# Both token halves of a tile multiplied together, block by block, into two PSUM banks in turn

## What is computed

```
z = rmsnorm(x) @ w_in                      # 1024 -> 7 x 1024: u, v, B, C, h, gate_a, gate_b
v = layernorm(gelu(v));  a = gelu(u) * (tril(w_s[g]) mixed over 128 positions of v + b_s[g])
bconv = B * causal_conv3(C * h)
m = sigmoid(gate_a) * (a @ w_pa) + sigmoid(gate_b) * (bconv @ w_pb)
x = x + m @ w_o
x = x + (silu(xn @ w_gate) * (xn @ w_up)) @ w_down     # xn = rmsnorm(x)
y = rmsnorm(x)
```

## Time and profile before

| | |
|---|---|
| median of 3 runs | 960.77 us (960.02 to 961.20) |
| span of the profiled execution | 959.0 us (its own device time is not shown apart) |
| TensorE busy (matmul) | 924.1 us, 96%, 7269 matmuls |
| TensorE weight loads | 919.4 us, 7269 loads |
| VectorE, ScalarE, GpSimd busy | 525.2 us, 259.3 us, 85.4 us |
| chain that ended last, by engine | PE 94%, DVE 3%, DMA 1% |

### The profile page before, as it was taken

The page is one execution under the profiler, slowest core; times in us unless marked ns, Lnnn a source line. Parts: engine busy times, 40 slices in busy tenths (PEclk is TensorE's granted clock), DMA queues, the critical chain, the costliest instruction groups (busy, mean ns, idle before and its releaser), DMA issues.

```text
span 959.0 us, 17757 instructions
## 1 busy us (share of the span) xinstructions
PE 924.1 (96%) x7269; PEld 919.4 (96%) x7269; DVE 525.2 (55%) x914; ACT 259.3 (27%) x378; POOL 85.4 (9%) x72
## 2 busy tenths in 40 slices
PE   6999499999998999999999999999999999999995
PEld 6998499999998999999999999999999999999995
DVE  4558965757577333355568755555533355555452
ACT  7333132223223333222211222222221222222331
POOL 0003610000004000000014300000000000000330
PEclk8999799999999999999999999999999999999997
DMA  9221122222121322222222222222234222221212
GB/s 311 91 88 46 44 89 89 89 84 85 55 87 51 125 89 87 88 88 87 82 94 85 83 69 86 85 83 78 63 94 129 91 88 86 87 71 55 83 55 94
DMA packets 90390, 84.27 MB, mean 88 GB/s; under 512 B 1596, under 2 KB 88724, under 8 KB 90356
## 3 DMA queue, kind: packets, MB, share of 16 engines
q1 hardware_dynamic: 90356, 83.81, 27.3%
HBM read 81.42 MB, written 2.38 MB: 87 GB/s over the span
## 4 chain that ended last, share of the span: by engine, by line
PE 94%; DVE 3%; DMA 1%; issue 1%; SPq 0%; ACT 0%; ACTq 0%; DVEq 0%
PE ps_main L416 30%; PE ps_main L414 30%; PE ps_main L415 30%; DVE w_lo L835 2%; DMA tok<-in_x_prompt_dram 1%; PE ps_g L526 1%; DVE tok L931 1%; PE ps_g L446 0%; PE ps_t L446 0%; DVE stats L903 0%; DVE tok L938 0%; PE ps_g L527 0%; PE ps_g L455 0%; PE ps_t L439 0%; DVE c_sb L842 0%
## 5 line engine op out<-in xcount | busy, mean ns | idle before, releaser
L414 PE MATMUL ps_main<-act_hi,w_hi 128*128 128x272 f32 x2336 | 677.8, 290 | 17.9 <-DVE xc L962 12.6
L416 PE MATMUL ps_main<-act_hi,w_lo 128*128 128x272 f32 x2336 | 678.9, 291 | 0.0
L415 PE MATMUL ps_main<-act_lo,w_hi 128*128 128x272 f32 x2336 | 674.1, 289 | 0.0
L414 PEld LDWEIGHTS ps_main<-act_hi,w_hi 128*128 128x128 f32 x2336 | 442.3, 189 | 19.1 <-DVE w_lo L835 12.8
L415 PEld LDWEIGHTS ps_main<-act_lo,w_hi 128*128 128x128 f32 x2336 | 442.9, 190 | 0.0
L416 PEld LDWEIGHTS ps_main<-act_hi,w_lo 128*128 128x128 f32 x2336 | 441.5, 189 | 0.0
L626 ACT CAST w_hi<-w_raw 128x2048 fp32r<-128x2048 f32 x50 | 95.3, 1906 | 285.0 <-PE ps_main L416 284.9
L829 DVE TENSOR_TENSOR w_lo<-w_raw,w_hi 128x2048 fp32r<-128x2048 f32 x50 | 127.8, 2556 | 48.3 <-ACT w_hi L626 48.1
L835 DVE SCALAR_TENSOR_TENSOR w_lo<-w_raw,g_cols,w_hi 128x256 fp32r<-128x256 f32 x224 | 100.0, 518 | 47.0 <-ACT w_hi L631 46.7
L631 ACT ACTIVATE w_hi<-w_raw,g_cols 128x256 fp32r<-128x256 f32 x224 | 92.5, 495 | 114.4 <-PE ps_main L416 114.0
L1119 DVE TENSOR_TENSOR gate_sb<-ps_main,r_all 128x544 f32<-128x544 f32 x22 | 15.9, 725 | 73.6 <-PE ps_main L416 73.3
(11 more groups left out here) (150 smaller groups left out, 401.1 us busy)
## 6 DMA issues: line engine op xcount, KB each, us to landing
w_raw<-in_w_in_dram SPq DMA_DIRECT2D x27, 1024.0 KB, 5.0
w_raw<-in_w_gate_dram SPq DMA_DIRECT2D x11, 1024.0 KB, 5.4
w_raw<-in_w_up_dram SPq DMA_DIRECT2D x11, 1024.0 KB, 5.3
w_raw<-in_w_down_dram SPq DMA_DIRECT2D x8, 768.0 KB, 4.7
w_raw<-in_w_down_dram SPq DMA_DIRECT2D x8, 640.0 KB, 4.3
w_raw<-in_w_pa_dram SPq DMA_DIRECT2D x4, 1024.0 KB, 4.9
w_raw<-in_w_pb_dram SPq DMA_DIRECT2D x4, 1024.0 KB, 4.9
w_raw<-in_w_o_dram SPq DMA_DIRECT2D x4, 1024.0 KB, 4.9
```

Of the source, the lines that this page charges most:

```text
L414: pe.matmul(out, whi, xhi, start=(k == 0), stop=False)
L415: pe.matmul(out, whi, xlo, start=False, stop=False)
L416: last = pe.matmul(out, wlo, xhi, start=False, stop=(k == blocks - 1))
```

## The change

unit no longer calls product_half for half 0 and then half 1. A new routine, product_both, goes over the K blocks once, and for each of the three products of a block it does half 0 and then half 1. Each of the two halves still has its own bank. Consecutive matmuls thus write the two banks of the pair in turn, and two in a row have the same weights. The waits ready(k, 0) and ready(k, 1) both stand before a K block. tile_half is raised by the last matmul of each half, which are now neighbours. The calls behind[i, 0] and behind[i, 1] both come after the whole tile. Phase "v" is left as it was.

```diff
--- before.py
+++ after.py
@@ -422,14 +422,32 @@
                 if p.name != "v" or s:
                     pe.wait_ge(dve_out[pair], p.out_before(j, s, i))
 
+            def product_both(p, j, s, i, blocks, x0, width, ready=None):
+
+                pair = p.pair(s, i)
+                for k in range(blocks):
+                    at = k * width + (i * P if p.per_unit == 2 else 0)
+                    whi = w_hi[:, s % 2, at:at + P]
+                    wlo = w_lo[:, s % 2, at:at + P]
+                    if ready is not None:
+                        ready(k, 0)
+                        ready(k, 1)
+                    for w, act in ((whi, act_hi), (whi, act_lo), (wlo, act_hi)):
+                        for h in range(2):
+                            last = pe.matmul(ps_main[:, pair, h, 0:HALF], w, act[:, x0 + k, h * HALF:(h + 1) * HALF],
+                                             start=(k == 0 and w is whi and act is act_hi),
+                                             stop=(k == blocks - 1 and w is wlo))
+                            if k == blocks - 1 and w is wlo:
+                                last.then_inc(tile_half, 1)
+
             def unit(p, j, s, x0, blocks=KD, ready=None, behind={}):
 
                 pe.wait_ge(lo_ready, p.unit(j, s))
                 for i in range(p.per_unit):
                     pair_free(p, j, s, i)
+                    product_both(p, j, s, i, blocks, x0, 2 * P if p.per_unit == 2 else P,
+                                 ready if i == 0 and s == 0 else None)
                     for h in range(2):
-                        product_half(p, j, s, i, h, blocks, x0, 2 * P if p.per_unit == 2 else P,
-                                     ready if i == 0 and s == 0 else None)
                         if (i, h) in behind:
                             behind[i, h]()
```

## The result

The changed kernel takes 962.95 us (median of 11 runs, 961.09 to 965.24) against 960.50 us for the kernel before, measured beside it (median of 11, 958.25 to 962.62). The ratio is 1.0028, with a 95% interval of 1.0019 to 1.0037: slower by 2.5 us, where 5.3 us had been forecast. The time is inside the forecast's range, and the loss is a little under half of what was forecast.

A forecast was written before the change was run, and what follows sets the result against it. TensorE, busy 96% of the span, was taken as the bound: matmul count times spacing, plus a few waits. 0 + 3.0 + 1.9 + 0.4 = 5.3 us on 959.0, plus 1.8 for the median, gave 966.1 us, range 959.5 to 971.5.

The forecast's parts named there:

- Term 2: Phase mix, first tile: transposes turn_v(7) come one half later, moving VectorE's chain and TensorE's restart; cost +3.0 us.
- Term 3: ffn_1, second tile: spread(), the norm's row factors, comes one half later against 1.19 us of slack; cost +1.9 us.
- Term 4: The end: the last tile's halves finish together, so TensorE's last sums wait longer for ScalarE's squares; cost +0.4 us.
- the rest is covered: Elsewhere, VectorE's later work on tiles (up to 2.2 us), norm_sums and the ready waits were to cost nothing.
- One sign: Sign in the profile after: TensorE's long wait, for xc, was to be 15.6 instead of 12.6 us.
- Term 1: Spacing of the 6624 reordered matmuls outside phase "v": no change, 0, +-3.6 us.
- the two bank-change steps: In ffn_2, steps from half 0 to half 1 and to the next tile: 0.13 us each, no shorter than ordinary 0.126.
- The bank turn pays: Rival: writing one bank repeatedly holds matmuls back; up to 83 us gained, 883 us, most of it near 957; chance 0.14.
- Each bank change costs: Rival: 13 ns paid at each bank change, up to 86 us, 1052 us; one tenth gives 975 us; chance 0.08.
- The clock falls: Rival: bank turning opens idle times, a tenth of products run at the lower clock, 67 us, 1033 us; chance 0.03.
- The moved parts cost nothing net: Rival: waits grow, but spacing 0.4 to 0.8 ns better per matmul pays for them; 961 us; chance 0.12.

## Why the prediction was wrong, point by point

**The direction and three of the four terms were right.** Term 2 (transposes, +3.0 us) shows as 5.2 us of wait for c_sb and a restart at 115.59, 2.8 us later; it costs 2.6 us by the difference of two timed kernels. Term 3 (spread, +1.9) shows as a 2.0 us wait and costs 2.4. Term 4 (+0.4) shows as 0.3 us of wait on x_last. That the rest is covered was right as well: there is no other new wait. One sign was wrong and does not enter the sum: the wait for xc could not grow by the same 3.0 us as the wait for c_sb, since the tile between them moves too.

**Term 1 failed, in its size.** It said "0, +-3.6 us"; measured are -3.7. The reasoning took the two halves' rates, 3.03 and 3.01 us, for properties that a mixed stream would average. The runs show that they belong to the place in SBUF from which the activations are read, and that the mixed order doesn't average them: turned at every matmul, all of it runs near the faster half's rate (6.013 a tile), turned in threes it runs as slowly as half 0's columns alone (6.053). The gain end of the stated range for this term, 3.6 us, is where the truth lay; the prediction named that case (the stream wholly at one half's rate) and took the middle without a row that shows a mixed stream.

That the time still lies within the range is in part luck. With the right term 1 the sum would have been 1.6 us; up to 1.6 us of lower clock behind the spread's wait, which the sum did not have, brought the time back towards the forecast. What was right in term 1 is the reading of the two bank-change steps: a change of bank as such brought no gain.

**The rivals.** "The bank turn pays" had a threshold of 0.8 ns a matmul; the order gave 0.56 (3.7 us / 6624), and not through the bank. "Each bank change costs" fell: in the changed kernel the bank turns at each matmul and a tile is shorter than before, and at half 1's columns it takes 6.000 us. "The clock falls" did not happen in the phases: in 18 tiles between 770.90 and 879.14 each takes 6.01 us, at a granted clock of 1.00. The Trainium skill ("TensorE: Matmul & The Clock Gate", A second HAM failure mode: psum-queue depth-cycling) tells of a bf16 kernel that cycles through banks, pauses between its groups of matmuls and loses the clock by it. Here the banks turn, no such pause and no lower clock appears in these tiles, and so its case is not this one. The clock did fall for one stretch, behind a wait for VectorE, worth 1.6 us; this the prediction had considered for the waits in "mix" and not for the new one. "The moved parts cost nothing net" was the nearest in mechanism: a better spacing paid for 3.7 of 5.3 us.

**In numbers:** 0 became -3.7, 5.3 stayed 5.3 (measured 5.0 for both hooks, 0.3 for the end), and the clock added up to 1.6, where the sum had 0.

## What to carry to other kernels

When a loop is turned inside out, look first at what was hung between its parts: here two small pieces of work moved by half a tile, 3 us, and cost more than the new order of products gained; put back, the same change was 3.4 us faster than the kernel before, and not 2.5 slower (some 0.7 of the 3.4 came with the unexplained 6.000 us tiles). Moving such work the other way, ahead of its old place, helps only until the next input is late: there 1.7 us earlier gave 0.3. And a rate that differs between two halves of a stream is a clue to be tested, not to be averaged: two runs, one that reads half 0's columns twice and one that reads half 1's, would have told which property it belongs to.

## What the runs showed of the hardware

- The spacing of fp32r matmuls with 272 columns and a weight load each is 125.0 to 126.1 ns in the steady phases, and depends on where the moving operand begins: 6.053 us in ffn_2 for 48 at columns 0 to 271, 6.009 at 16 to 287 and at 272 to 543, which both begin an odd multiple of 64 bytes further. Something else has a part in it: the same columns 0 to 271 take 6.027 in merge_b, and the order of the change takes 6.013 or 6.000 in different phases of one kernel. What it is was not found. Exchanging the two banks that are written changes nothing (3.034 and 3.006 us for the two halves, 3.033 and 3.007 before).
- Loading the same weights four times in a row is no faster than loading others (6.013 us both for four equal pairs in six and for one).
- A stretch at half clock came with or right behind a wait of 2.0 us on TensorE in four of nine profiled kernels (some 3.5 us long), one of 2.2 to 2.3 us in five of eight, one of 3.0 to 3.2 us (for sig) in fifteen of seventeen, and one of 5.1 to 5.2 us in all eight. One such stretch behind the spread's wait costs 1.6 us. Single runs of the changed kernel differ by 4.2 us; the slowest, 965.24 us, has the lowest mean granted clock, 0.976 against 0.979 to 0.982 of the others. That these stretches are the cause of the differences is likely by this, and was not tried.
